# An encoder layer on one core: two first tiles computed chunk by chunk inside the norms before them, the convolution's norm sums and the final norm reordered

## What is computed

```
hn   = rmsnorm(x) * g * (1 + sc1) + sh1                 # sh, sc, g.. = silu(c) @ ada + b
proj = hn @ w_in          # 7 groups of 512: q, ff, fb, i, g of the recurrence, a and gate of the convolution
o_h  = bidirectional gated recurrence(q, ff, fb, i), rms-normed per head, * silu(g)
o_c  = silu(layernorm(depthwise_conv31(a * sigmoid(gate)) + bias))
h1   = x + g1 * (concat(o_h, o_c) @ w_out)
hn2  = rmsnorm(h1) * g * (1 + sc2) + sh2
q    = hn2 @ wq ; two score sets of 128 keys per head, 8 heads ; top 16 of the pair sums
y    = sum over 8*16 chosen experts of softmax * gelu(hn2 . u[e]) * v[e]
out  = rmsnorm(h1 + g2 * y) * g * (1 + fsc) + fsh
```

## Time and profile before

| | |
|---|---|
| median of 3 runs | 3167.31 us |
| profiled execution: its own time / its span | 3162.14 / 3160.4 us |
| TensorE busy | 2901.7 us (92%) |
| VectorE busy | 2270.6 us (72%) |
| ScalarE / GpSimd busy | 845.7 / 1234.6 us |
| bytes moved | 919.80 MB, mean 291 GB/s |
| mean granted TensorE clock | 0.953 |

### The profile page before, as it was taken

The page is one execution under the profiler, slowest core; times in us unless marked ns, Lnnn a source line. Parts: engine busy times, 40 slices in busy tenths (PEclk is TensorE's granted clock), DMA queues, the critical chain, the costliest instruction groups (busy, mean ns, idle before and its releaser), DMA issues. The chain is left out here.

```text
span 3160.4 us, 31542 instructions
## 1 busy us (share of the span) xinstructions
PE 2901.7 (92%) x10300; PEld 1568.6 (50%) x10300; DVE 2270.6 (72%) x4432; ACT 845.7 (27%) x1683; POOL 1234.6 (39%) x1101
## 2 busy tenths in 40 slices
PE   6999699879699999799999999996999999999995
PEld 2557477767475544345454444452444444444442
DVE  4696454561577789999788888875676766767775
ACT  3111533431221101355366566581000000000003
POOL 0111110121134545444444444545554565655661
PEclk8998899979898999899999999998999999999997
DMA  4441110122237999999999998999999999999994
GB/s 177 174 160 65 53 34 27 34 81 104 77 99 293 412 415 394 341 385 374 366 335 372 346 369 317 415 415 406 403 401 407 401 405 400 401 397 402 401 402 183
DMA packets 285837, 919.80 MB, mean 291 GB/s; under 512 B 25840, under 2 KB 75248, under 8 KB 278256
## 3 DMA queue, kind: packets, MB, share of 16 engines
q0 software_dynamic: 147456, 536.94, 43.6%
q1 hardware_dynamic: 99584, 301.75, 25.3%
q10 hardware_dynamic: 38640, 79.18, 6.5%
HBM read 830.21 MB, written 87.56 MB: 290 GB/s over the span
## 5 line engine op out<-in xcount | busy, mean ns | idle before, releaser
L1525 PE MATMUL s_pu<-s_hn,s_ut 128*128 128x512 f32 x2304 | 1012.5, 595 | 4.7 <-ACT s_gst L1637 4.7
L1919 DVE SCALAR_TENSOR_TENSOR s_hB<-s_slot,s_dot,s_hB 128x1024 f32<-128x1024 f32 x469 | 596.2, 1284 | 262.4 <-DMA s_slot<-in_v,s_row 259.7
L1480 POOL DMA_INDIRECT s_slot<-in_v,s_row x512 | 586.4, 1145 | 429.8 <-DVE s_hB L1919 318.0
L1480 POOL DMA_INDIRECT s_slot<-in_u,s_row x512 | 502.0, 980 | 642.7 <-DVE s_slot L1905 557.3
L1525 PEld LDWEIGHTS s_pu<-s_hn,s_ut 128*128 128x128 f32 x2304 | 434.8, 191 | 531.2 <-issue 530.6
L1905 DVE SCALAR_TENSOR_TENSOR s_slot<-s_slot,s_ph 128x1024 f32<-128x1024 f32 x512 | 610.2, 1219 | 82.7 <-DMA s_slot<-in_u,s_row 63.3
L302 PE MATMUL s_ps<-hn_hi,w_hi 128*128 128x512 f32 x704 | 289.5, 411 | 81.1 <-PEq L276 40.3
L1690 ACT ACTIVATE s_hotw<-s_hot,s_rest 128x128 bf16<-128x128 bf16 x1024 | 308.5, 423 | 52.6 <-ACT s_gst L1637 25.5
L1611 PE MATMUL s_pw<-s_ct,s_vt 128*128 128x512 f32 x512 | 248.1, 608 | 47.1 <-DVE s_ct L1927 29.4
L303 PE MATMUL s_ps<-hn_lo,w_hi 128*128 128x512 f32 x704 | 281.2, 399 | 0.0
L1744 ACT ACTIVATE y<-s_pw 128x512 f32<-128x512 f32 x2 | 1.2, 597 | 929.9 <-PE s_pw L1611 929.9
(11 more groups left out here) (286 smaller groups left out, 2877.0 us busy)
## 6 DMA issues: line engine op xcount, KB each, us to landing
s_ut<-in_u_tiles SPq DMA_DIRECT2D x128, 512.0 KB, 7.2
s_vt<-in_v_tiles SPq DMA_DIRECT2D x32, 2048.0 KB, 19.4
s_g<-s_gst ACTq DMA_DIRECT2D x128, 256.0 KB, 7.0
s_w<-s_wb ACTq DMA_DIRECT2D x16, 2048.0 KB, 11.4
s_gr<-s_g SPq DMA_DIRECT2D x64, 512.0 KB, 27.6
s_wr<-s_w SPq DMA_DIRECT2D x16, 2048.0 KB, 29.4
s_ada<-in_ada SPq DMA_DIRECT2D x48, 512.0 KB, 5.2
s_ada<-in_ada SPq DMA_DIRECT2D x4, 2048.0 KB, 20.3
```

What stands on the lines that cost most here:

```text
L1480: pool.indirect_dma_start(out=slot[s][:, :], out_offset=None, in_=io[kind], in_offset=bass.IndirectOffsetOnAxis(ap=row[b][:, j:j + 1], axi ...
L1525: mm = pe.matmul(pu[:, n % 2, :], ut[n % UR][:, k, :], hn[:, k, :], start=(k == 0), stop=(k == DC - 1))
L1919: dve.scalar_tensor_tensor(y, s, dot[b][:, j:j + 1], y, ALU.mult, ALU.add).then_inc(taken, 1)
```

## The change

1. **step1 and step2.** Two PSUM pairs `m.ps` are held from step1 through step2. At the end of step1 TensorE runs the first gate tile and the first value tile, chunk by chunk as `hn_lo` of each chunk is ready, and step2 starts without them.
2. **End of step2.** TensorE makes three head tiles, then the means and the variance sums, and only then the fourth head tile and the columns of the six vectors. The root is taken before the inverse, straight from PSUM (one VectorE operation less), and the drains between the mean subtractions are gone.
3. **step4 and step5.** The first two query tiles are run in step4, chunk by chunk behind `hn_lo`.
4. **step6 and step8.** step8 is gone; its work stands at the end of step6, by token halves (h=1 dense, h=0 sparse), in 128x512 operations. `h1` is read in four DMAs of 2 KB rows while the last `v` tiles run. The residual of the dense half reads the PSUM banks directly, so the eight copies to `y` are gone. Outputs leave in 16 DMAs of 256 KB.

```diff
 def step1  # tensor, after the columns of s_mod
             pe.drain().then_inc(mod_ready, 1)
+            pe.wait_ge(w_split, 2)
+            for k in range(DC):
+                pe.wait_ge(lo_ready, k + 1)
+                for s in range(2):
+                    project(pe, ps[s], m.w_hi[s], m.w_lo[s], m.hn_hi, m.hn_lo, (k,))
+            pe.drain()
 def step2  # tensor
             w.begin(pe)
+            pe.sem_inc(w.used, 2)
             for c in range(CONV_C):
-                w.ready(pe, c, 0)
-                pe.wait_ge(sig_ready, c + 1)
-                project(pe, ps[0], ...).then_inc(w.used, 1)
...
+                if c:
+                    w.ready(pe, c, 0)
+                    pe.wait_ge(sig_ready, c + 1)
+                    project(pe, ps[0], ...).then_inc(w.used, 1)
...
                 ada_rows(range(c * A_PER, (c + 1) * A_PER))
-            for n in range(4):
-                (head tile n)
+            for n in range(3):
+                head_tile(n)
             pe.wait_ge(row_taken, 6)
-            (48 columns into ps_var) ; pe.drain().then_inc(mod_ready, 1)
-            (means of the four chunks)
+            means(range(CONV_C - 1))
+            means((CONV_C - 1,)).then_inc(mu_ready, 1)
             (variance sums) ; pe.drain().then_inc(var_ready, 1)
+            head_tile(3)
+            pe.wait_ge(evac, 3)
+            columns(range(6))
+            pe.drain().then_inc(mod_ready, 1)
 def step2  # scalar
-            for n in range(2):
-                take(2 + n)
-                w.round(act, CONV_C + 2, n)
+            take(2)
+            w.round(act, CONV_C + 2, 0)
...
-            act.activation(r[:, :], r[:, :], ACT.Sqrt).then_inc(r_ready, 1)
+            act.wait_ge(var_ready, 1)
+            act.activation(r[:, :], ps_var[:, :], ACT.Sqrt, scale=1.0 / DCONV, bias=m.eps[:, 0:1]).then_inc(r_ready, 1)
             (four times SiLU, drain, store)
+            w.round(act, CONV_C + 2, 1)
+            take(3)
 def step4  # tensor, after the sums of squares
+            for s in range(2):
+                w.ready(pe, DC // 2, s)
+            for k in range(DC):
+                pe.wait_ge(y_lo, k + 1)
+                for s in range(2):
+                    project(pe, ps_q[s], w.hi[s], w.lo[s], m.hn_hi, m.hn_lo, (k,), (0,))
+            pe.drain()
 def step5  # tensor
+            pe.sem_inc(w.used, 2)
+            for s in range(2):
+                scores(pe, 0, s)
-            with pe.Fori(0, PH) as h:
+            with pe.Fori(1, PH) as h:
 def step6  # sync
-            sp.wait_ge(v_done, KEYS)
-            sp.dma_start(m.h1_back[:, :, :], m.h1.rearrange("k p t -> p k t")).then_inc(h1_in, 16)
+            sp.wait_ge(product, KEYS - 4)
+            (three DMAs: chunks 0-3, 4-5, 6-7 of the dense half).then_inc(dense_in, 16)
+            sp.wait_ge(product, KEYS)
+            sp.dma_start(h1_sparse[:, :, :], back[:, :, 0:HALF]).then_inc(sparse_in, 16)
+            for h in (1, 0):
+                for k in range(DC):
+                    sp.wait_ge(done[h], k + 1)
+                    sp.dma_start(io["out"][k][:, h * HALF:(h + 1) * HALF], y[:, h, k, :]).then_inc(stored[h], 16)
 def step6  # tensor
-            pe.wait_ge(kept, DC)
+            pe.wait_ge(taken, SPARSE_OPS)
+            pe.wait_ge(h2_ready[1], 4)
+            for b in range(2):
+                turn_y(b)
+            pe.wait_ge(h2_ready[1], 6)
+            squares(1, range(4))
+            for b in range(2, SPARSE):
+                pe.wait_ge(y_out, b - 1)
+                turn_y(b)
+            squares(1, range(4, DC))
+            pe.wait_ge(h2_ready[1], DC)
+            squares(0, range(DC))
 def step6  # scalar
+            square(1, range(4))
+            for b in range(SPARSE):
+                take_turned(b)
+            square(1, range(4, DC))
+            root_of(1)
+            square(0, range(DC))
+            root_of(0)
+            (16 times: wait xn_ready, add the shift).then_inc(done[h], 1)
 def step6  # vector, after the last gathered row
+            dve.wait_ge(dense_in, 16 * len(h1_dense))
+            for k in range(DC):
+                dve.wait_ge(made, k + 1)
+                residual(1, k)
+            dve.wait_ge(sparse_in, 16)
+            dve.wait_ge(y_out, SPARSE)
+            for k in range(DC):
+                residual(0, k)
+            invert(1)
+            invert(0)
+            dve.drain()
+            for h in (1, 0):
+                for k in range(DC):
+                    dve.scalar_tensor_tensor(y[:, h, k, :], y[:, h, k, :], m.mods[:, 7, k:k + 1], spread[h][:, :], ALU.mult,
+                                             ALU.mult).then_inc(xn_ready[h], 1)
```

More of the change, by code:

```diff
@@ L990, in step4 @@
         ps = m.ps
+        ps_q = m.ps_q = [m.hold.enter_context(nc.psum_tensor(f"s4_q{s}", [P, HALF], F32)) for s in range(2)]
         ps_ss = ctx.enter_context(nc.psum_tensor("s4_ss", [P, T], F32))
@@ L1081, in _ @@
                 remainder(k)
-    m.hold.close()
 def step5(nc, m, io, sem):
@@ L2025, with residual @@
-STEPS = (step1, step2, step3, step4, step5, step6, step8)
-def encoder_layer(nc, io, out, steps=7, scratch="Internal"):
+                while asked < sparse_by_v(n):
+                    sparse(asked)
+                    asked += 1
+            def residual(h, k):
+                part = h1_sparse[:, k, :] if h == 0 else (h1_dense[0][:, k, :] if k < 4 else h1_dense[k // 2 - 1][:, k % 2, :])
+                dve.scalar_tensor_tensor(y[:, h, k, :], bank(k) if h else y[:, 0, k, :], m.mods[:, 5, k:k + 1], part,
+                                         ALU.mult, ALU.add).then_inc(h2_ready[h], 1)
```

217 lines of the change are left out of this document (97 added, 120 removed).

## The result

| | before | after |
|---|---|---|
| median of 4 runs | 3168.34 us (3166.84 to 3170.92) | 3136.91 us (3134.47 to 3140.36) |
| ratio, 95% interval | | 0.9909 (0.9896 to 0.9921) |
| profiled execution, span | 3162.14, 3160.4 us | 3134.47, 3132.8 us |

The changed kernel is faster by 31.4 us by the medians and by 27.7 us between the two profiled executions (the one of before lies 6.2 us under its median, the one of after 2.4 under its own). The forecast was 36.1 us: 3131.2, range 3121 to 3150.

A forecast was written before the change was run, and what follows sets the result against it. Steps are separated by barriers, each bounded by the engine its barrier waits for. Gains of 24.3 (step1, step2), 4.5 (step4, step5) and 7.3 (tail) sum to 36.1 us: 3167.3 to 3131.2, range 3121 to 3150.

The forecast's parts named there:

- Part 1, the tiles and the convolution: Step1 and start of step2: tiles start at 64.4, VectorE's first gate product comes 10.0 us earlier, last tap at 284.6.
- Part 1, the rows: Start of step2: TensorE's first 12 vector rows wait for memory and end at 111.8 instead of 122.46, gaining 10.7 us.
- Part 2: End of step2: last mean sum waits only for VectorE; step3 starts at 328.7, 24.3 us earlier including the earlier start.
- the 2 us I had put in for it: Variance sums at the end of step2: 2 us added because TensorE may restart at the low clock.
- The rival of a low clock through the whole norm: End of step2: means, variance and fourth tile at 1.2 GHz, costing 13 us there; 3150 in all, chance 0.10.
- Part 3: Step4 and step5: head 1's tile ends at 853.8 instead of 858.35, gaining 4.5 us, bounds 1 and 6.5.
- The rival that I weighed there: Step4: chunks shorter than their waits all run slow, 2.6 us each; gain 0.5 instead of 4.5 us, no chance given.
- Part 4: Tail: last gathered row added 7.0 us later, then 45 us to the end, a gain of 7.3 us.
- the 3.1 us taken off for the dips and for VectorE's trailing: Tail: 10.2 us of added bytes reduced by 2.1 for traffic dips and about 1 for VectorE's trailing, giving 7.0 us.
- the tail gives nothing: Tail: `h1` bytes delay gathers by 13 us or low clock holds in the sums; 28.8 us remain, 3138.5, chance 0.14.

The follow-up runs named there:

- f1: The changed kernel with the first gate and value tile run in step2 again: 3144.31 us, ratio 0.9925 to the kernel before.
- f4: The changed kernel with the first five modulation rows read in step1 into a buffer: 3132.98 us, ratio 0.9896 to the kernel before.
- f2: The changed kernel with the end of step2 in the old order (four head tiles, columns, means, variance): 3157.53 us, ratio 0.9968 to the kernel before.
- t1: The changed kernel with all `h1` reads issued only after the last `v` tile: 3132.13 us, ratio 0.9887 to the kernel before.
- t3: The changed kernel with every byte of `h1` read twice: 3144.98 us, ratio 0.9934 to the kernel before.
- f5: The changed kernel with the first two query tiles run in step5 again: 3143.31 us, ratio 0.9925 to the kernel before.
- f3: The changed kernel with six columns issued behind each chunk of the fourth head tile: 3133.05 us, ratio 0.989 to the kernel before.
- best2: The changed kernel with late sparse `h1` read, one half scaled first, four columns behind each fourth-tile chunk, sixteen behind the tile: 3127.11 us, ratio 0.9862 to before.

## Why the forecast was right, and where it was short

The sign and the range held, and so did most of the mechanism; one step of it failed, and two sizes were off. Of the 36.1 us, the traces show 27.7. The missing 8.4 are four things: 3.1 in step1 and step2, 2.6 in the tail, 3.4 in stages that the change does not touch, less 0.6 that step4 and step5 gave beyond the forecast (8.5 with rounding). All stage figures are of one execution each. The 3.4 lie within what untouched stages vary by, and so would most of the 3.1: with the scan at 331.3 to 335.5 the gain of the front is 20.4 to 24.6 us, 24.3 forecast. Of the tail's 2.6 not so: over the six traces with that tail the gain is 2.0 to 4.7 us, never the 7.3.

- **Part 1, the tiles and the convolution: right.** Start 64.44, first product 92.52 (91.7 forecast), last tap 285.7 (284.6). f1 shows its worth on VectorE's chain, 9.9 us, of which 2.0 are a late start of that trace.
- **Part 1, the rows: the step that failed, at little cost.** "TensorE has to do the first 12 vector rows alone, and they now wait for memory: [...] 111.8", a gain of 10.7 us. The term left out is TensorE's own time: a row is four records of 0.43 us, so 12 rows are 48 records and 20.6 us. The earlier trace rows showed it: 101.50 to 122.46 is 21.0 us for those rows with their data present. Memory, with its 18 to 19 us, was never the longer of the two; it only decides when the first row is there (97.60; f4, with the rows at hand, starts at 91.21 and ends them at 113.86). 97.60 and 20.6, and 1.9 for the slow clock in which they start, are the 120.1. TensorE gained 2.4 us (f2: 2.6).
- **Part 2: right in mechanism, 3.1 us short.** The means ended at 289.8 instead of 286.5. The failed step alone does not explain this: f4 gives TensorE 6.2 of the missing 8.3 us back, and the means end at 289.84 all the same. The tap ended 1.1 us later than forecast, and the last four records, put at 1.9 us behind it, took 3.35 in f4 and 3.55 in f1: behind the wait the clock falls to half as they start. Had the rows gone as forecast, that size would have been short instead. The slow clock in the variance (8.64 us for 16 records that take 7.13 before, in t1, t3 and f4) cost 1.5 of the 2 us I had put in for it, and the fourth tile, columns and barrier together took 31.0 us against 30.6. The rival of a low clock through the whole norm did not come: the means ran at full rate, 7.03 us.
- **Part 3: right.** 5.1 us net, 4.5 forecast; f5 isolates 5.2. The rival that I weighed there did not come: the granted clock stood at 0.50 up to 807, while the first chunks followed each other without a gap, and then stayed at 1.00 over the other chunks of step4, with TensorE busy 6.13 of 8 us. The case of the Trainium skill ("TensorE: Matmul & The Clock Gate", section "HAM oscillation — how this bites in real kernels") is a group of matmuls shorter than the wait behind it, and I had applied it where it doesn't reach. Here, by the prediction's own figures, 1.4 us of work stand against 1.0 us of waiting, and the trace has waits of 0.40 and 0.73 us; it neither bears that rule out nor speaks against it.

```profile
804.00:807.00 3.00, 3.00 (x8) 2.30 (x8) 3.00 (x4) 1.70 (x2) 0.00 (x0) 0.50 0.00 0
808.00:816.00 8.00, 6.13 (x25) 4.07 (x24) 8.00 (x8) 3.45 (x3) 0.00 (x0) 1.00 0.01 2
```

- **Part 4: length right, delay too small.** The chain behind the last gathered row is 45.1 us, as summed. The gathers were delayed by 9.5 us, not 7.0. The 10.2 us of bytes at 410 GB/s were the right start, and nearer to the mean of the seven lags (10.1, 10.8 later than before); the 3.1 us taken off for the dips and for VectorE's trailing were not there. VectorE trails the traffic as before: the last bytes flow just behind 3084 and its additions end at 3087.64; before, they flowed up to some 3097 and the additions ended at 3101.05. The rival "the tail gives nothing" was half right: the read is not hidden at all, as t1 shows; what remains, 4.7 us here and 3.1 in the mean of six traces, is the lost barrier and the halved first wait. `h1`'s reads slow the gathers as soon as they are issued: from 3010 to 3030 us the gathers moved 6.54 MB, and from 3032 to 3052, behind the read's issue at 3031.48, 5.46 MB, while the other queue went from 0.92 to 2.57 MB. This agrees with what the Trainium skill states in "DMA: Bandwidth & Descriptors", section "Queues, rings and completion order", that a memory engine serves the queues for which it has work in turn. The order of the packets themselves no run here shows.

## To carry to other kernels

Before a chain is said to wait for memory, divide the old trace's own time of it by its count: the longer of the two terms counts, and it often stands in the row already read. Two chains that end close together must be shortened together; alone, these two parts gave 2.2 and 11.3 us, and together 21.2. A read that is issued early is not hidden where the memory is already busy (here at some 400 GB/s); the free place for it was where the windows show no traffic, behind the work that it was meant to precede. And where two chains end close together, an error in one of them hardly shows in the time: here the trace and f4 told it.

## What was not expected of the hardware

- **The clock falls under one-column matmuls; mixed with wide ones it does not.** In the changed kernel the 96 records of columns begin at full clock and end at half (granted clock 0.97 in the first window below, 0.50 in the second, with TensorE busy in both), 17.42 us in all. So it is in every trace that has them in one piece, 16.2 to 17.4 us. Behind chunks of 128x512 matmuls the same records run at 0.124 us each, 11.9 us, with the clock at 1.00 from 302 to 326 us (f3). In `best2` the 32 records that stand together take 0.156 us each.

```profile
312.00:316.00 4.00, 4.00 (x35) 3.81 (x34) 1.34 (x2) 3.14 (x3) 0.00 (x0) 0.97 0.80 320
316.00:320.00 4.00, 4.00 (x20) 4.00 (x20) 0.00 (x0) 2.23 (x3) 2.13 (x1) 0.50 0.52 209
```

- **A wait of a few microseconds before a short group of sums can cost as much as it saves.** The last four mean records take 3.35 us behind 4.58 us of idle time (f4) and 3.55 behind 4.17 (f1), where 16 take 7.03 without a pause (1.8 us for four).
- **Untouched stages move by 8 to 10 us from one execution to another of nearly the same program** (step3 364.1 to 371.8, step6 2150.1 to 2160.3). What moves them was not traced.
